# Row maximum carried in a spare contraction row of the second score pass

## The reference, cut to what matters

```python
def _masked_probs(s, mask):
    s = jnp.where(mask, s, NEG)
    m = jnp.max(s, axis=-1, keepdims=True)
    p = jnp.where(mask, jnp.exp(s - m), 0.0)
    return p / jnp.maximum(jnp.sum(p, axis=-1, keepdims=True), TINY)
...
    s = jnp.einsum('btgrd,bgtmd->bgrtm', qg, ks).astype(jnp.float32) * SCALE
    p = _masked_probs(s, mask)
    return jnp.einsum('bgrtm,bgtmd->btgrd', p, vs)
...
    s = jnp.einsum('btgrd,bkgd->bgrtk', qg, kw).astype(jnp.float32) * SCALE
    p = _masked_probs(s, mask)
    return jnp.einsum('bgrtk,bkgd->btgrd', p, vw)
```

## Time and profile before

| | |
|---|---|
| runs | 1236.37, 1239.74, 1241.45 us, median 1239.74 |
| profiled execution | 1240.48 us, span 1238.8 us, mean granted clock 0.981 |
| TensorE matmul busy | 1170.1 us, 94% |
| VectorE busy | 504.3 us, 41% |
| ScalarE busy | 371.8 us, 30% |
| GpSimd busy | 467.4 us, 38% |

### The profile page before, as it was taken

The page is one execution under the profiler, slowest core; times in us unless marked ns, Lnnn a source line. Parts: engine busy times, 40 slices in busy tenths (PEclk is TensorE's granted clock), DMA queues, the critical chain, the costliest instruction groups (busy, mean ns, idle before and its releaser), DMA issues.

```text
span 1238.8 us, 20877 instructions
## 1 busy us (share of the span) xinstructions
PE 1170.1 (94%) x8574; PEld 1064.2 (86%) x8574; DVE 504.3 (41%) x646; ACT 371.8 (30%) x497; POOL 467.4 (38%) x257
## 2 busy tenths in 40 slices
PE   6899998999999999898999879999999999999996
PEld 5899998999999897565565449999999999999994
DVE  5585673043312222778882433454322322300115
ACT  5112433233111124444433222333332322322211
POOL 5332544565434431027411033434434434434440
PEclk9899999999999999999999899999999999999997
DMA  5432126323622210930106272232232233222201
GB/s 171 157 100 69 51 82 207 103 84 93 212 71 82 88 41 21 301 115 18 35 19 214 62 249 82 88 103 85 86 102 92 77 102 100 69 94 94 93 25 69
DMA packets 108785, 124.10 MB, mean 100 GB/s; under 512 B 10478, under 2 KB 102662, under 8 KB 107455
## 3 DMA queue, kind: packets, MB, share of 16 engines
q1 hardware_dynamic: 105544, 118.61, 30.5%
q10 hardware_dynamic: 3191, 4.80, 1.2%
HBM read 111.38 MB, written 16.17 MB: 103 GB/s over the span
## 4 chain that ended last, share of the span: by engine, by line
PE 75%; issue 13%; POOL 5%; DVE 4%; DMA 2%; ACT 1%; POOLq 0%; DVEq 0%; SPq 0%; ACTq 0%
PE D L1672 54%; PE E L1672 6%; PE D L1920 5%; POOL w_lo L692 4%; PE D L1906 1%; PE E L1993 1%; PE D L1907 1%; PE D L1908 1%; DVE nmax L1399 1%; DMA w_raw<-in_w_in 1%; PE E L1891 1%; PE E L1934 1%; PE E L1986 1%; PE D L1868 1%; PE D L2027 0%
## 5 line engine op out<-in xcount | busy, mean ns | idle before, releaser
L692 POOL TENSOR_TENSOR w_lo<-w_raw,w_hi 128x1024 fp32r<-128x1024 f32 x164 | 402.7, 2478 | 569.5 <-ACT w_hi L770 522.5
L770 ACT ACTIVATE w_hi<-w_raw 128x1024 fp32r<-128x1024 f32 x164 | 164.2, 1050 | 288.6 <-PE D L1672 244.2
L1672 PE MATMUL D<-hH,w_hi 128*128 128x260 f32 x1152 | 235.7, 286 | 7.7 <-POOL w_lo L692 5.5
L1672 PE MATMUL D<-hH,w_lo 128*128 128x260 f32 x1152 | 234.2, 285 | 0.0
L1672 PE MATMUL D<-hL,w_hi 128*128 128x260 f32 x1152 | 233.9, 285 | 0.0
L1672 PEld LDWEIGHTS D<-hH,w_hi 128*128 128x128 f32 x1152 | 180.2, 191 | 8.3 <-POOL w_lo L692 5.7
L1672 PEld LDWEIGHTS D<-hL,w_hi 128*128 128x128 f32 x1152 | 179.8, 191 | 0.0
L1672 PEld LDWEIGHTS D<-hH,w_lo 128*128 128x128 f32 x1152 | 179.8, 191 | 0.0
L1672 PE MATMUL D<-onH,w_hi 128*128 128x260 f32 x832 | 167.6, 283 | 1.1 <-DVE onL L1579 1.1
L1672 PE MATMUL D<-onH,w_lo 128*128 128x260 f32 x832 | 167.7, 283 | 0.0
L1672 PE MATMUL D<-onL,w_hi 128*128 128x260 f32 x832 | 167.4, 283 | 0.0
(11 more groups left out here) (347 smaller groups left out, 1562.6 us busy)
## 6 DMA issues: line engine op xcount, KB each, us to landing
w_raw<-in_w_in SPq DMA_DIRECT2D x64, 512.0 KB, 5.0
w_raw<-in_w_ffn_in SPq DMA_DIRECT2D x44, 512.0 KB, 4.0
slot<-in_cache_kv SPq DMA_DIRECT2D x64, 128.0 KB, 2.9
w_raw<-in_w_ffn_out SPq DMA_DIRECT2D x16, 512.0 KB, 4.3
rows_b<-rnorm_d SPq DMA_DIRECT2D x8, 512.0 KB, 4.6
w_raw<-in_w_nsa_out SPq DMA_DIRECT2D x8, 512.0 KB, 7.0
slot<-in_cache_win SPq DMA_DIRECT2D x16, 256.0 KB, 4.0
w_raw<-in_w_o SPq DMA_DIRECT2D x8, 512.0 KB, 3.9
```

The lines of the kernel that those rows point to most:

```text
L692: nc.gpsimd.tensor_tensor(wl[b][:, x], raw[b][:, x], wh[b][:, x].bitcast(F32), ALU.subtract)\
L770: nc.scalar.activation(wh[b][:, x], raw[b][:, x], ACT.Copy).then_inc(hi_done, 1)
L1672: ins = mm(out2[:, a, 0:HALF], lhsT, rhs[:, a * HALF:(a + 1) * HALF], start=first, stop=last)
```

## The change

The diagonal matrices and their pass (L1908) go. The negative maximum becomes one row of the contraction of the second pass. That pass no longer multiplies by `qst` but by a new `qmx`: one partition half holds the high part of the queries (copied there by a transfer, 512 KB a group), the other half is zero but for two rows, one for each branch, with the maxima of the group. `k2` keeps the low part of the keys in its own half; the other half is zero but for a row of ones where the branch's maximum lies. (The product of both low parts is left out by this.) The maxima get into that row form by TensorE: after eight of the 16 row scores it turns [128 x 16] maxima into 16 rows in an unused part of an `E` bank, VectorE copies them to `nmaxT`, and a transfer takes eight rows of 128 into one row of `qmx`; two halves and two branches make four transfers a group, issued by ScalarE. `qmx` lies where `xT` and the selected values of the cache lay, so the load of these goes behind the loop. GpSimd clears the halves and writes the ones before the loop. Staging moves to tiles 0 to 3 (ScalarE) and 1 to 3 (VectorE), the row maxima to tiles 5 to 14. Of the eight compressed tiles two come between the first group's row scores and two behind them. Seven semaphores are merged into others.

```diff
+T_MAX = 15
...
+        def max_row(g, br):
+            return (1 - g % 2) * DH + 32 * br
+        def max_rows(eng, g, a):
+            eng.wait_ge(nmax_out, 2 * g + a + 1)
+            for br in range(2):
+                o = max_row(g, br)
+                row = qmx[g % 2][o:o + 1, 2 * a:2 * a + 2, :, :].bitcast(F32).rearrange("o q r x -> o (q r) x")
+                eng.dma_start(row, nmaxT[g % 2][a][br * 8:br * 8 + 8, :]).then_inc(qmx_max[a], 16)
...  SyncE: own_q(sp, u // 2 + 1) ahead of an even branch's sums
+            def own_q(eng, g):
+                eng.wait_ge(q_hi, 4 * g + 2)
+                if g >= 2:
+                    eng.wait_ge(scores_done, 2 * NT * (g - 1))
+                h = slice(g % 2 * DH, (g % 2 + 1) * DH)
+                eng.dma_start(qmx[g % 2][h, :, :, :].bitcast(F32), qst[g % 2][h, :, :, :].bitcast(F32)).then_inc(qmx_q, 16)
...
-            sp.wait_ge(x_kept, 16)
-            rows(3, range(NS))
+            sp.wait_ge(scores_done, STEPS)      # behind the loop over the branches
+            rows(3, range(NS))
...  GpSimd, before the values are staged, for b in 0, 1
+                nc.gpsimd.memset(qmx[b][other, :, :, :].bitcast(F32), 0.0).then_inc(qmx_clear, 1)
+                nc.gpsimd.memset(k2[b][other, :, :].bitcast(F32), 0.0).then_inc(qmx_clear, 1)
+                for br in range(2):
+                    nc.gpsimd.memset(k2[b][o:o + 1, br, :].bitcast(F32), 1.0).then_inc(qmx_clear, 1)
...
         def max_step(n):
-            return 8 + n * 12 // 16
+            return 5 + n * 10 // 16
...  ScalarE
+                if n == 4:
+                    act.dma_start(qmx[0][half(0), :, :, :].bitcast(F32), qst[0][half(0), :, :, :].bitcast(F32)).then_inc(qmx_q, 16)
+            for a in range(2):
+                max_rows(act, 0, a)
-                g, n = t // (2 * NT) + 1, t % (2 * NT) - 3
+                if t < LAST and t % (2 * NT) == T_MAX - 3:
+                    max_rows(act, t // (2 * NT) + 1, 0)
+                if t < LAST and t % (2 * NT) == T_MAX + 1:
+                    max_rows(act, t // (2 * NT) + 1, 1)
+                g, n = t // (2 * NT) + 1, t % (2 * NT)
...  VectorE: stage_lo at t % 20 = 1 to 4 (n == 3 returns), diagonal() gone
+            def turned_max(g, a):
+                dve.wait_ge(nmax_turned, 2 * g + a + 1)
+                nc.vector.tensor_copy(nmaxT[g % 2][a][:, :], E[0:4 * R, 3 - 2 * a, 384:512]).then_inc(nmax_out, 1)
...  TensorE
+            def turn_max(g, a):
+                pe.wait_ge(nmax_done, 16 * g + 8 * a + 8)
+                turn(E[0:4 * R, 3 - 2 * a, 384:512], nmax[:, g % 2, a, :, :, :].rearrange("p b q r -> p (b q r)"),
+                     ident[:, :]).then_inc(nmax_turned, 1)
+                if n % 16 == 8:                 # in row_scores(n)
+                    turn_max(g, 0)
+                if n % 16 == 9:
+                    pe.wait_ge(nmax_out, 2 * g + 1)
-                if kt == 0:
-                    pe.wait_ge(dm_ready, i + 1)
+                if t % (2 * NT) == 0:
+                    pe.wait_ge(qmx_q, 16 * g + 16)
+                    pe.wait_ge(qmx_max[0], 32 * g + 32)
+                if t % (2 * NT) == 3:
+                    pe.wait_ge(qmx_max[1], 32 * g + 32)
-                mm(out, k2[b][:, br, ks], q, start=False, stop=False)
-                mm(out, ones_r[:, :], dm[i % 3][:, :, :], start=False, stop=True).then_inc(scores_done, 1)
+                mm(out, k2[b][:, br, ks], qmx[b][:, qi, :, :].rearrange("p r x -> p (r x)"), start=False, stop=True).then_inc(scores_done, 1)
+                        if t % (2 * NT) == T_MAX:    # in the loop, behind the row scores
+                            turn_max(g, 1)
```

More of the change, by code:

```diff
@@ L216, in build @@
         obuf = [over(f"obuf{b}", [P, R, SEQ]) for b in range(2)]
-        dm = [over(f"dm{b}", [P, R, P], F32R) for b in range(3)]
+        nmaxT = [[over(f"nmaxT{b}{a}", [4 * R, P]) for a in range(2)] for b in range(2)]
+        nmax = over("nmax", [P, 2, 2, 2, 2, R])
+        over.off += 3 * size([P, R, P]) - 4 * size([P, P]) - size([P, 2, 2, 2, 2, R])
         kvc_off = over.off
@@ L222, in build @@
         rnorm = [over(f"rnorm{b}", [P, SEQ // 32]) for b in range(2)]
-        nmax = over("nmax", [P, 2, QT, 2, R])
+        over = Region(base, w_off)
+        qmx = [over(f"qmx{b}", [P, QT, R, P], F32R) for b in range(2)]
         over = Region(h_off, h_off + size([P, R, SEQ]))
@@ L377, in build @@
         nmax_done = sem("nmax_done")
-        dm_ready = sem("dm_ready")
+        qmx_clear = sem("qmx_clear")
+        qmx_q = sem("qmx_q")
+        nmax_turned = sem("nmax_turned")
+        nmax_out = sem("nmax_out")
+        qmx_max = [sem(f"qmx_max{a}") for a in range(2)]
         scores_done = sem("scores_done")
@@ L1398, in row_max @@
                 dve.wait_ge(max_mm, n + 1)
[L1399 to L1410, removed]
+                a = qi // 2
+                if g >= 2:
+                    dve.wait_ge(nmax_turned, 2 * (g - 2) + a + 1)
+                nc.vector.reduce_max(nmax[:, g % 2, a, :, qi % 2, h], src, AX.X, negate=True).then_inc(nmax_done, 1)
+            def turned_max(g, a):
+                dve.wait_ge(nmax_turned, 2 * g + a + 1)
+                if g >= 2:
+                    dve.wait_ge(qmx_max[a], 32 * (g - 1))
+                nc.vector.tensor_copy(nmaxT[g % 2][a][:, :], E[0:4 * R, 3 - 2 * a, 384:512]).then_inc(nmax_out, 1)
             def normalizer(u):
@@ L1439, in _ @@
                 row_max(n)
-                if n == 3:
-                    diagonal(0)
+                if n % 8 == 7:
+                    turned_max(0, n // 8)
             dve.wait_ge(cmp_evac, KT)
@@ L1796, in _ @@
             ins.then_inc(tails_turned, 1)
[L1797 removed]
+            pe.wait_ge(v_lo, WT + 1)
             with pe.Fori(C_MIX2 // 2, C_Q // 2) as i:
@@ L1864, in _, with cmp_tile @@
                 pe.wait_ge(tile_free[m], 1 + C_NSA)
-            for ft in range(KT):
+            def cmp_tile(ft):
                 if ft >= 4:
@@ L1921, in value_tile @@
                    start=(kt == 0), stop=(kt == qi)).then_inc(pv_done, 1)
+            for ft in range(4):
+                cmp_tile(ft)
+            pe.wait_ge(kv_evac, 12)
+            pe.wait_ge(kvs_evac, 3)
             for n in range(16):
                 row_scores(n)
+                if n in (11, 13):
+                    cmp_tile((n - 3) // 2)
+            cmp_tile(6)
+            cmp_tile(7)
+            turn_max(0, 1)
             pe.wait_ge(cmp_evac, KT)
```

84 lines of the change are left out of this document (48 added, 36 removed).

## The result

The changed kernel takes 1230.38 us (median of five runs, 1227.87 to 1232.20) against 1239.74 (1236.37 to 1241.45): ratio 0.9927, 95% interval 0.9904 to 0.9950. So it is faster, by 9.4 us (0.8%); 1230.0 was forecast. The profiled execution took 1231.63 (span 1229.9), 8.9 less in span than the one before.

What follows compares the result with a forecast made beforehand. TensorE's own order of work was taken as the bound up to tile 70. Group gains of -2.6, 6.5, 4.3 and 2.3, together 10.5 us, off the profiled 1240.48 gave 1230.0; range 1219 to 1240.

Steps and rivals of the forecast that it cites:

- The pass: Attention tiles: removing the 0.23 us pass takes 16.1 us off TensorE over 70 tiles.
- VectorE's lag: Row maxima in ten tiles: the turn waits for VectorE 0.7, 3.9 and 2.5 us in groups one to three.
- Last ten tiles free: Last ten tiles of the loop: they don't count, since what follows hangs on SyncE's chain, not on TensorE.
- Staging at tiles 0 to 3: Group's first tiles: one VectorE staging operation (1.22) goes, the rest ends before the normalizer, 8.9 us of waits go.
- Row maxima and diagonals: Row maxima at tiles 5 to 14: about 2.5 us a group of wait; 32 diagonals, 26.6 us, go from VectorE.
- Sizes: Second and third groups: first row scores wait 0.3 us for VectorE, a value product 1.5 for a late eviction.
- Start: Start of the loop: tile 0 waits for turn, copy, two issues and a landing, starting near 516.0, 5.4 us later.
- The clock behind tile 0: Wait before tile 0, about 3 us of idle: a clock that falls again there would add 1 to 2 us.
- TensorE alone: Second and third groups: banks hide VectorE's lag and the late eviction, 34.55 us each, 1220 in all; chance 0.25.
- late transfers in the loop: Tile 3 of each group: TensorE waits for late row transfers, slower, 1253 at twice the slowest landing; chance 0.1.
- that rival: VectorE becomes the bound: second group 48.8 us, 2.1 longer than before, 1238.6 in all; chance 0.2.

Runs made afterwards that it cites:

- the schedule alone: Kernel before the change with only the change's staging and row-maxima places, three score passes and diagonals kept: 1243.89 us, ratio 1.0016.
- the old schedule: Changed kernel with staging back at tiles 3 to 6 (ScalarE) and 4 to 7 (VectorE), row maxima at tiles 8 to 18: 1231.34 us, ratio 0.9913.
- the kernel with spread maxima: Changed kernel with row maxima over tiles 5 to 17, second turn at 17, row transfers at 14 and 18: 1231.51 us, ratio 0.9935.
- the kernel with two edits: Changed kernel with the first pair of row transfers issued early and SyncE's two loads behind the last two branches' rows: 1220.60 us, ratio 0.9835.
- the early pair: Changed kernel with the first group's first pair of row transfers issued ahead of ScalarE's last four compressed tiles: 1223.96 us, ratio 0.9877.

## Why the prediction was right, and where not

The total and the starts of the tiles came out, in part by luck (below): second group 552.76 (forecast 551.9), 39.14 and 39.12 for the next two (40.2 and 38.9), ten tiles of the fourth 2.32 shorter (2.3), 10.45 at tile 70 (10.5). Behind it the profiled execution lost 1.55; over the experiments that leave it alone that stretch spans 571.7 to 577.0, so the 1.55 can't be told from scatter.

- *The pass:* right, and only with the waits. The forecast took 16.1 and gave 7.1 back for VectorE's lag (0.7, 3.9 and 2.5), net 9.0; put back, it costs 10.0 to tile 70.
- *Last ten tiles free:* right. The sums of the seventh branch are issued 7.86 us behind the start of tile 70 now (661.93) and 8.81 before (673.33), and land 14.70 and 14.50 behind it: what TensorE gains there is lost in SyncE's queue, and its wait for the key products grows from 2.4 to 4.8. Moving the loads that stand ahead of those sums is worth as much as most of the change.
- *Staging at tiles 0 to 3:* this step failed. "The 8.9 us of waits go" was right, the cause not: the schedule alone left 10.6, and without it they went all the same. Under the old schedule they went because VectorE has one staging operation fewer, the one that stood behind the normalizer; I had priced it at 1.22 and put the wait's end down to the new place. With three passes, the diagonals and all four operations, the new place leaves as much waiting as the old one. In the new place that operation was not put back alone: the diagonals alone bring these waits from 3.2 to 4.5, the third pass alone to 2.4, so that it makes most of the 10.6 there too is likely and not shown.
- *Row maxima and diagonals:* VectorE's lag is there, 1.1 us a turn and slower tiles ahead of it, and the 26.6 us of diagonals that I called gone from VectorE without a price are worth 6.6. GpSimd's products beside the second group, for which I added 1.4, cost about 1.0: GpSimd was busy 16.1 of 23 us beside the row maxima there and 2.7 of 20 in the third, and tiles 26 to 36 take 23.10, tiles 46 to 56 22.12. That the two groups are equal is chance: the third loses 1.0 more at its eviction and first row scores (tiles 44 and 45).
- *Sizes:* the first row scores wait 1.45 and 1.7 (forecast 0.3), because VectorE works off the branch before between the staging operations; tiles 24 and 44 take 0.6 and 1.3 more than 1.33 (forecast 1.5). The misses cancel, which is luck.
- *Start:* from the second turn to tile 0 it is 3.78, and copy, two issues and a landing were forecast at 3.8, but that is luck: tile 0 waits for the first pair alone, which was turned at 500.81 and stood on ScalarE behind the last compressed tile (513.35), not behind the second turn and its copy. The forecast's own terms, 512.6 and 3.8, give 516.4 and not the 516.0 that it went on with. From the first row scores to tile 0 19.4 were forecast; 19.3 are measured at full clock (494.98 to 514.32, the kernel with spread maxima) and 21.6 where it fell. The row scores began 1.3 earlier than forecast (495.31), so tile 0 at 516.93 is two misses that cancel.
- *The clock behind tile 0:* it fell as feared, 0.65 from tile 0 to tile 6, which took 9.88 (forecast 9.0); at 1.00, in the kernel with two edits, it is 9.06. So its price was about 0.8, a little less than the 1 to 2 that the prediction allowed for.
- *Rivals:* TensorE alone (34.55 a group) is refuted by the waits, late transfers in the loop by the old-schedule run. VectorE does set the pace in half of each group, but not to the extent of that rival.

The parts don't add: fourth operation 9, pass 10, diagonals 6.6, each put back alone, are more than the 16.8 that the groups gained. A slower TensorE hides VectorE's work and the other way round: ten of the passes cost 0.9 beside the row maxima.

## What to carry to other kernels

When a wait ends with an engine's last operation, count the operations ahead of it before moving the group: one fewer in a full queue was worth 8 to 9 us in three groups, moving all four nothing. A small transfer on the critical path should be issued as soon as its data is there and ahead of any megabytes, on its own queue (2.13 in place of 6.84) or on another engine's (some 7 us with the early pair); two such edits and one that moved work into idle time gave 12 us on top of the change (1217.14 against 1229.10). An operation's price depends on which engine sets the pace of its stretch: the same 0.23 us pass counted in full in ten tiles and for 0.09 in ten others.

## What was not expected of the hardware

The granted clock fell between 500 and 510 us in some executions (0.66, 0.70) and not in others (1.00) of the same instructions, and moved tile 0 by 2.3 us. An issue of a row transfer took ScalarE longer than the one row of before, 476 ns; the issues of the changed kernel by line, and the first four on its timeline, behind the last compressed tile:

```profile
L452 ACTq DMA_DIRECT2D qmx<-nmaxT x16: 627/627/772, 513.4 to 627.5; - x16
```

```profile
513.35 0.60 ACT L956 ACTIVATE onT<-D 128x512 f32<-128x512 f32 x1 [0.26 <-PE D L1917]
513.41 2.77 ACTq L452 DMA_DIRECT2D qmx<-nmaxT  x4
```

Two of the four were out by 514.8 (half of 2.77), and tile 0 began 2.1 later, beside SyncE's running loads; the 8 KB of sums took 6.84 behind SyncE's own 4 MB. By the Trainium skill (DMA: Bandwidth & Descriptors, "Queues, rings and completion order") a DMA engine takes turns between the queues that it has work for. The landing at 514 doesn't tell such turns from one common order, since SyncE's own loads landed in 2.7 us there. The prediction took from ScalarE's own queue that a backlog of SyncE's would not count. The run with the early pair speaks against that: the first packet of ScalarE's rows ran 4.6 us or more after the first issue, and the last some 7 us after the issues, like the loads beside them. What held them up is open.
